# The triangular inverse of a gated delta rule: X of each level as a transpose of XT

## The chip, the core and the metric

The kernel runs on one core of one Trainium2 chip. The metric is the device time of one execution in microseconds; the lower, the better. Three runs of the kernel before gave 1061.08 to 1063.31 us with a median of 1063.28 us.

## What is computed

Two transformer blocks in a row on 256 tokens of width 1024, all in float32. The first has sliding-window attention beside a recurrent unit and a feed-forward part. The second has a block-sparse attention (8 heads) beside a gated delta rule (8 heads of 128), and again a feed-forward part. The change lies in the gated delta rule alone. The reference splits the 256 tokens into chunks of 64; the kernel uses two chunks of 128, which gives the same function. What matters of the reference:

```python
def gated_delta_rule(q, k, v, g, beta):
    ...
    gc = jnp.cumsum(g, axis=-1)
    decay = jnp.exp(jnp.where(causal, gc[..., :, None] - gc[..., None, :], -jnp.inf))
    k_beta = k * beta[..., None]
    a_low = jnp.where(strict, jnp.einsum("bhnid,bhnjd->bhnij", k_beta, k) * decay, 0.0)
    t_mat = a_low + jnp.eye(L, dtype=f32)
    rhs = jnp.concatenate([v * beta[..., None], k_beta * jnp.exp(gc)[..., None]], axis=-1)
    sol = lax.linalg.triangular_solve(t_mat, rhs, left_side=True, lower=True, unit_diagonal=True)
    u = sol[..., :dv]
    w = sol[..., dv:]
    attn = jnp.where(causal, jnp.einsum("bhnid,bhnjd->bhnij", q, k) * decay, 0.0)
    ...
```

## The kernel before

It is written engine by engine; each engine runs its own program in order and waits on semaphores. Weights come from memory in panels of 1 MB through a ring of four slots, two units of 128x1024 to a panel. For float32 accuracy every weight unit is split into two parts that TensorE multiplies at its fast rate: ScalarE copies the high part (`hi`, L601), VectorE subtracts it to get the low part (`lo`, L1044). A unit of projection is eight steps of three matmuls each (L1497 to L1499 or L1503 to L1505). When TensorE has finished a unit, ScalarE copies its result out of PSUM (L800 for the first six of a round) and splits the unit four further on, and VectorE makes that one's low part.

The delta rule has four rounds, one for each pair of heads (`a` = 0 to 3, called first to fourth round here). A round has 21 stages, written by hand for each engine (`gdn_stage`). Between the stages stand projection steps for the next round (for the last: for a gate), as many behind each stage as the table `GDN_WEAVE` says: 9, 8, 4, 6, 4, then one behind each of stages 5 to 16, then 4, 3, 3 and 11. ScalarE and VectorE handle unit `c` behind the stage in which its eighth step falls: unit 3 in stage 5, unit 4 in stage 13, unit 5 in stage 18, none in stages 14 to 17.

The solve is done as a triangular inverse. X is the inverse of (A + 1) for blocks on the diagonal, for four matrices of 128x128 (two chunks, two heads) at once, and XT is its transpose. Level 0 starts in stage 3. Levels 1 to 6 take two stages each and double the blocks:

- odd stage (5, 7, ... 15), "P": TensorE forms A transposed times XT (L1799), two matrices to a group `g`; VectorE masks the result into PM (L1324).
- even stage (6, 8, ... 16), "Z": TensorE forms X transposed times PM (L1810), and in levels 1 to 5 also PM transposed times X (L1814), a third product. VectorE subtracts half of the first from XT and half of the second from X (`grow`, L1289). The next P waits for XT, the next Z for X and PM.

Other work stands in the same stages. ScalarE: `out_root` (the root of the output norm of the round before, L909 to L912) in stage 7, `decays` of the next round (L898, L901, L902) in stage 13, `out_hi` (L917) in stage 14, the gate's silu (L888, with a load of its function table) in stage 15, and then the copies between the state products: u0 (L870, stage 17), S1 (L873), vn (L876), o (L891). VectorE: `prepare` (L1344, L1346) in stage 8, `exponents` (L1350, L1351) in stage 10, `out_rows` (L1358, L1360) in stage 11, `out_lo` (L1366) in stage 14. TensorE: `g_rows` (L1855) in stage 9, `out_transposes` (L1861) in stage 13, the products with X (L1820, L1822) in stage 17, and L1827 in stage 18, which waits for u0. The convolution of the next round runs on POOL (L564, L567) behind the raw copies. `gdn_stage` has the new lines at the stages named.

Of the kernel before, what the change touches and what calls it, by code (L numbers as in the profile page):

```python
# [26 lines left out]
ACT = mybir.ActivationFunctionType  # L27
AX = mybir.AxisListType.X

P = 128  # L30
# [14 lines left out]
PAIRS = HEADS2 // 2  # L45
# [159 lines left out]
def build(nc, A):  # L205
    ctx = ExitStack()
    with ctx:
# [3 lines left out]
        def sem(name):  # L211
            return ctx.enter_context(nc.semaphore(name))
# [27 lines left out]
        def carve(state, *shape):  # L240
# [149 lines left out]
            sem(n) for n in ("gdn_v_rows", "gdn_k_rows", "gdn_kk_products", "gdn_kq_products", "gdn_attn_ready", "gdn_q_scaled", "gdn_kv_scaled", "gdn_A_ready", "inv_identity_ready",  # L390
                             "inv_x0_ready", "inv_xt0_in_psum", "inv_xt0_ready"))

        lv_p, lv_pm, lv_z, lv_x, lv_xt = ([sem(f"{n}{g}") for g in range(2)] for n in (
            "inv_p_in_psum", "inv_p_ready", "inv_z_in_psum", "inv_x_ready", "inv_xt_ready"))
        vb_out, sz_out, os_out = sem("gdn_vb_ready"), sem("gdn_gate_ready"), sem("gdn_o_copied")
        uw_ps, u0_out, nw_out, so_ps, S1_out, vn_ps, vn_out, o_ps, og_out, y_out, yT_ps, yb_hi, yb_lo = (
            sem(n) for n in ("gdn_u_w", "gdn_u0", "gdn_nwT", "gdn_state_ps", "gdn_state", "gdn_vnew_ps", "gdn_vnew",
# [184 lines left out]
        def _(act):  # L582
# [255 lines left out]
            def gdn_stage(s, a):  # L838
# [35 lines left out]
                if s == 19:  # L874
                    act.wait_ge(vn_ps, a + 1)
                    act.activation(vn, acc[:, 3, 256:512].rearrange("p (j n) -> p j n", j=2), ACT.Copy).then_inc(vn_out, 1)  # L876
                if s == 7 and not (isinstance(a, int) and a == 0):
                    out_root(a - 1)
                if s == 14 and not (isinstance(a, int) and a == 0):
                    out_hi(a - 1)  # L880
                if s == 13 and not (isinstance(a, int) and a == PAIRS - 1):
                    decays(a + 1)
                if s == 15:
                    act.wait_ge(emptied[0], along(EMPTIED0, 2 * P_GDN + 8, 8, a))
                    act.wait_ge(emptied[1], along(EMPTIED1, 2 * P_GDN + 8, 8, a))
                    if not (isinstance(a, int) and a == 0):
                        act.wait_ge(y_out, a)
                    act.activation(sz, zr, ACT.Silu).then_inc(sz_out, 1)  # L888
# [16 lines left out]
            def out_root(b):  # L905

                act.wait_ge(os_out, b + 1)
                for pr in range(4):
                    ins = act.activation(junk[:, 512 + pr * P:640 + pr * P], o_s[:, pr, :], ACT.Square, accum_out=st[:, pr:pr + 1])  # L909
                ch.link(ins)  # L910
                ch.link(act.activation(st[:, 4:8], st[:, 0:4], ACT.Ln, bias=eps[:, 0:1], scale=1.0 / P))
                act.activation(st[:, 4:8], st[:, 4:8], ACT.Exp, scale=-0.5).then_inc(og_out, 1)  # L912
# [116 lines left out]
        def _(dve):  # L1029
# [253 lines left out]
            def half_blocks(x, n, odd):  # L1283

                return x.rearrange("p r (q two b) -> p (r q) two b", two=2, b=1 << n)[:, :, odd, :]

            def grow(x, n, odd, z):
                v = half_blocks(x, n, odd)
                return TT(v, v, z, ALU.subtract)  # L1289

            def gdn_stage(s, a):
# [34 lines left out]
                if 5 <= s < 17 and s % 2 == 0:  # L1326
                    lv = (s - 5) // 2 + 1
                    for g in range(2):
                        dve.wait_ge(lv_z[g], a * 6 + lv)
                        z = acc[:, 1 + g, :].rearrange("p (r n) -> p r n", r=4)  # L1330
                        grow(XT_[:, 2 * g:2 * g + 2, :], lv, 1, half_blocks(z[:, 0:2, :], lv, 1)).then_inc(lv_xt[g], 1)
                        if lv < 6:
                            grow(X_[:, 2 * g:2 * g + 2, :], lv, 0, half_blocks(z[:, 2:4, :], lv, 0)).then_inc(lv_x[g], 1)
                if s == 17:
                    dve.wait_ge(uw_ps, a + 1)
                    TS(nwT, acc[:, 0, 0:256].rearrange("p (j n) -> p j n", j=2), -1.0, None, ALU.mult).then_inc(nw_out, 1)
# [146 lines left out]
        def _(pe):  # L1483
# [273 lines left out]
            def gdn_stage(s, a):  # L1757
# [30 lines left out]
                if 5 <= s < 17 and s % 2 == 1:  # L1788

                    lv = (s - 5) // 2 + 1  # L1790
                    if lv == 1:
                        pe.wait_ge(xt0_out, a + 1)
                        pe.wait_ge(kv_out, a + 1)
                        pe.wait_ge(attn_out, a + 1)
                    for g in range(2):
                        if lv > 1:
                            pe.wait_ge(lv_xt[g], a * 6 + (lv - 1))
                        for j in range(2):
                            last = mm(acc[:, 3 * g, j * P:(j + 1) * P], A_[:, 2 * g + j, :], XT_[:, 2 * g + j, :], start=True, stop=True)  # L1799
                        last.then_inc(lv_p[g], 1)  # L1800
                if 5 <= s < 17 and s % 2 == 0:

                    lv = (s - 5) // 2 + 1
                    for g in range(2):
                        pe.wait_ge(lv_pm[g], a * 6 + lv)
                        if lv > 1:
                            pe.wait_ge(lv_x[g], a * 5 + (lv - 1))
                        for j in range(2):
                            pr = 2 * g + j
                            last = mm(acc[:, 1 + g, j * P:(j + 1) * P], X_[:, pr, :], PM_[:, pr, :], start=True, stop=True)  # L1810
                        if lv < 6:
                            for j in range(2):
                                pr = 2 * g + j
                                last = mm(acc[:, 1 + g, (2 + j) * P:(3 + j) * P], PM_[:, pr, :], X_[:, pr, :], start=True, stop=True)  # L1814
                        last.then_inc(lv_z[g], 1)
                if s == 17:
                    for g in range(2):
# [154 lines left out]
```

## Time and profile before

| | |
|---|---|
| median of three runs | 1063.28 us (1061.08 to 1063.31) |
| span of the profiled execution | 1062.7 us; only the span is recorded for it, 0.6 us under the median |
| TensorE busy | 933.3 us (88%), 6486 instructions |
| VectorE busy | 580.4 us (55%) |
| ScalarE busy | 515.9 us (49%) |
| POOL busy | 139.2 us (13%) |
| mean granted TensorE clock | 0.949 |
| the four rounds | about 520 to 738 us from the span's start, 54 us each |

Each row of a timeline has the start in us from the span's start, the duration, engine, line, operation, output and inputs, shape and the number of merged instructions. The bracket is the idle time of that engine before it and what ended it. A float32 matmul of 128x128 leaves two records, a float32 transpose one. Matmuls are pipelined: a group's printed duration has the tail of its last one in it, so the distance between starts says what a group occupies. All tiles carved out of one large buffer are called R, PSUM is ps.

### The profile page before, as it was taken

The numbers are of one execution on the slowest core, as the hardware profiler recorded it, in microseconds if no ns is written. First come the engines' busy times: TensorE is split into PE (matmuls) and PEld (weight loads), VectorE is DVE, ScalarE is ACT, GpSimd is POOL, SyncE is SP. The second block draws the span as 40 slices with busy tenths as digits, with TensorE's granted clock in tenths as the row PEclk, the third lists the DMA queues.
The fourth block names the chain that finished last, engine by engine and source line by source line (L and its number), as shares of the span: only waits on it lengthen the run. The fifth ranks groups of instructions, "written<-read, shape, count | busy, mean of one in ns | idle before, by whom it ended". The sixth has DMA issues, their size and how long they took to land.

```text
span 1062.7 us, 16705 instructions
## 1 busy us (share of the span) xinstructions
PE 933.3 (88%) x6486; PEld 856.1 (81%) x6486; DVE 580.4 (55%) x842; ACT 515.9 (49%) x859; POOL 139.2 (13%) x131
## 2 busy tenths in 40 slices
PE   1598769999999789988699898998988999999967
PEld 1596548999897788988688888888976799999946
DVE  1376554555556555558463737363656455555454
ACT  2458453444445544555636464636336444444442
POOL 4000021000000000007555545300000000000000
PEclk9699889999999889999899999999989899999969
DMA  9643227565556244444122222222554465555601
GB/s 191 210 160 119 79 57 158 188 197 193 169 192 198 75 131 152 124 152 144 62 73 84 76 80 79 80 80 80 180 188 134 142 192 170 194 197 170 231 34 39
DMA packets 106876, 144.88 MB, mean 136 GB/s; under 512 B 3104, under 2 KB 94368, under 8 KB 106704
## 3 DMA queue, kind: packets, MB, share of 16 engines
q1 hardware_dynamic: 104304, 137.37, 40.7%
q0 software_dynamic: 2208, 6.25, 2.8%
q10 hardware_dynamic: 320, 0.66, 0.2%
q8 instruction: 30, 0.49, 0.2%
q14 instruction: 14, 0.11, 0.0%
HBM read 143.22 MB, written 1.05 MB: 136 GB/s over the span
## 4 chain that ended last, share of the span: by engine, by line
PE 73%; DVE 11%; ACT 9%; DMA 3%; issue 3%; POOL 1%; SPq 0%; ACTq 0%; DVEq 0%; POOLq 0%
PE ps L1497 13%; PE ps L1499 13%; PE ps L1498 13%; PE ps L1503 8%; PE ps L1505 8%; PE ps L1504 8%; DVE wl L1044 3%; DMA w_raw<-in_w_in_dram 3%; ACT wh L601 3%; PE ps L1799 2%; PE ps L1810 1%; DVE xTl L1072 1%; PE ps L1688 1%; PE ps L1814 1%; PE ps L1631 1%
## 5 line engine op out<-in xcount | busy, mean ns | idle before, releaser
L1044 DVE TENSOR_TENSOR wl<-w_raw,wh 128x1024 fp32r<-128x1024 f32 x258 | 322.8, 1256 | 354.8 <-ACT wh L601 354.2
L1497 PE MATMUL ps<-xTh,wh 128*128 128x256 f32 (+1 forms) x1160 | 339.2, 292 | 29.3 <-DVE xTl L1072 20.3
L601 ACT ACTIVATE wh<-w_raw 128x1024 fp32r<-128x1024 f32 x258 | 270.5, 1052 | 133.1 <-PE ps L1505 85.7
L1498 PE MATMUL ps<-xTl,wh 128*128 128x256 f32 (+1 forms) x1160 | 329.2, 284 | 0.0
L1499 PE MATMUL ps<-xTh,wl 128*128 128x256 f32 (+1 forms) x1160 | 328.9, 284 | 0.0
L1497 PEld LDWEIGHTS ps<-xTh,wh 128*128 128x128 f32 x1160 | 222.4, 192 | 34.1 <-DVE xTl L1072 20.7
L1498 PEld LDWEIGHTS ps<-xTl,wh 128*128 128x128 f32 x1160 | 221.3, 191 | 2.6 <-issue 1.7
L1499 PEld LDWEIGHTS ps<-xTh,wl 128*128 128x128 f32 x1160 | 222.2, 192 | 0.0
L1503 PE MATMUL ps<-wh,y 128*128 128x512 f32 x224 | 88.9, 397 | 4.0 <-DVE y L1452 4.0
L1505 PE MATMUL ps<-wh,y 128*128 128x512 f32 x224 | 88.6, 395 | 0.0
L1504 PE MATMUL ps<-wl,y 128*128 128x512 f32 x224 | 88.1, 393 | 0.0
L564 POOL TENSOR_TENSOR R<-R 128x512 f32<-128x512 f32 x12 | 13.2, 1103 | 390.6 <-ACT R L800 390.6
L1503 PE MATMUL ps<-wh,xTh 128*128 128x256 f32 (+3 forms) x184 | 56.9, 311 | 7.6 <-DVE xTl L1072 2.7
L1504 PE MATMUL ps<-wl,xTh 128*128 128x256 f32 (+3 forms) x184 | 55.4, 303 | 0.0
L564 POOL TENSOR_TENSOR gain<-R 128x512 f32<-128x512 f32 x36 | 54.9, 1524 | 2.8
L1505 PE MATMUL ps<-wh,xTl 128*128 128x256 f32 (+3 forms) x184 | 55.2, 302 | 0.0
L1503 PEld LDWEIGHTS ps<-wh,y 128*128 128x128 f32 x224 | 42.8, 191 | 12.3 <-DVE y L1452 4.3
L1505 PEld LDWEIGHTS ps<-wh,y 128*128 128x128 f32 x224 | 42.6, 190 | 9.5
L1504 PEld LDWEIGHTS ps<-wl,y 128*128 128x128 f32 x224 | 42.7, 191 | 8.4
L567 POOL TENSOR_TENSOR R<-R,gain 128x512 f32<-128x512 f32 x36 | 43.6, 1210 | 2.8
L1503 PEld LDWEIGHTS ps<-wh,xTh 128*128 128x128 f32 (+1 forms) x184 | 34.7, 189 | 10.9 <-issue 5.5
L752 ACT ACTIVATE R<-ps 128x256 f32<-128x256 f32 x32 | 12.3, 383 | 59.6 <-PE ps L1499 59.6
(331 smaller groups left out, 1337.7 us busy)
## 6 DMA issues: line engine op xcount, KB each, us to landing
w_raw<-in_w_in_dram SPq DMA_DIRECT2D x43, 1024.0 KB, 5.2
w_raw<-in_w_ff_dram SPq DMA_DIRECT2D x32, 1024.0 KB, 5.4
w_raw<-in_w_ffn_gate_dram SPq DMA_DIRECT2D x11, 1024.0 KB, 5.3
w_raw<-in_w_ffn_up_dram SPq DMA_DIRECT2D x11, 1024.0 KB, 5.4
w_raw<-in_w_ffn_down_dram SPq DMA_DIRECT2D x11, 1024.0 KB, 4.9
w_raw<-in_w_out_dram SPq DMA_DIRECT2D x8, 1024.0 KB, 4.8
w_raw<-in_w_proj_a_dram SPq DMA_DIRECT2D x4, 1024.0 KB, 5.0
w_raw<-in_w_proj_b_dram SPq DMA_DIRECT2D x4, 1024.0 KB, 4.9
```

Source lines behind the costliest of these rows:

```text
L564: ins = pool.tensor_tensor(cvt if tap else y, x, w, ALU.mult)
L567: ins = pool.tensor_tensor(y, y, cvt, ALU.add)
L601: act.activation(split_view(wh, pu % UNITS, layout), raw_unit(SLOT[p], j, layout), ACT.Copy).then_inc(w_hi, 1)
L752: act.activation(hid_t[:, j, :], fm[:, j, 0:S], ACT.Relu).then_inc(emptied[j], 1)
L1044: TT(split_view(wl, pu % UNITS, layout), raw_unit(SLOT[p], j, layout), split_view(wh, pu % UNITS, layout).bitcast(F32), ALU.subtract).then ...
L1497: mm(out, wh_, xh, start=first, stop=False)
L1498: mm(out, wh_, xl, start=False, stop=False)
L1499: return mm(out, wl_, xh, start=False, stop=last)
L1503: mm(out, xh, wh_, start=first, stop=False, skip_group_check=not group)
L1504: mm(out, xh, wl_, start=False, stop=False, skip_group_check=not group)
L1505: return mm(out, xl, wh_, start=False, stop=last, skip_group_check=not group)
L1799: last = mm(acc[:, 3 * g, j * P:(j + 1) * P], A_[:, 2 * g + j, :], XT_[:, 2 * g + j, :], start=True, stop=True)
```

## The change

In levels 1 to 5 the third product (PM transposed times X) and VectorE's update of X are gone. Instead TensorE, in the odd stages of levels 2 to 6 behind the P products, transposes the four matrices of XT into the half of the PSUM bank that the third product used, two to a semaphore, and ScalarE copies each group of two into X, 128x256 at a time; Z of that level waits for the copy as it waited for the update. On ScalarE three steps move to make room: `out_root` from stage 7 to stage 4, `decays` from 13 to 16, the silu from 15 to 16, behind the decays.

```diff
--- before.py
+++ after.py
@@ -390,8 +390,8 @@
             sem(n) for n in ("gdn_v_rows", "gdn_k_rows", "gdn_kk_products", "gdn_kq_products", "gdn_attn_ready", "gdn_q_scaled", "gdn_kv_scaled", "gdn_A_ready", "inv_identity_ready",
                              "inv_x0_ready", "inv_xt0_in_psum", "inv_xt0_ready"))
 
-        lv_p, lv_pm, lv_z, lv_x, lv_xt = ([sem(f"{n}{g}") for g in range(2)] for n in (
-            "inv_p_in_psum", "inv_p_ready", "inv_z_in_psum", "inv_x_ready", "inv_xt_ready"))
+        lv_p, lv_pm, lv_z, lv_t, lv_x, lv_xt = ([sem(f"{n}{g}") for g in range(2)] for n in (
+            "inv_p_in_psum", "inv_p_ready", "inv_z_in_psum", "inv_x_in_psum", "inv_x_ready", "inv_xt_ready"))
         vb_out, sz_out, os_out = sem("gdn_vb_ready"), sem("gdn_gate_ready"), sem("gdn_o_copied")
         uw_ps, u0_out, nw_out, so_ps, S1_out, vn_ps, vn_out, o_ps, og_out, y_out, yT_ps, yb_hi, yb_lo = (
             sem(n) for n in ("gdn_u_w", "gdn_u0", "gdn_nwT", "gdn_state_ps", "gdn_state", "gdn_vnew_ps", "gdn_vnew",
@@ -874,13 +874,18 @@
                 if s == 19:
                     act.wait_ge(vn_ps, a + 1)
                     act.activation(vn, acc[:, 3, 256:512].rearrange("p (j n) -> p j n", j=2), ACT.Copy).then_inc(vn_out, 1)
-                if s == 7 and not (isinstance(a, int) and a == 0):
+                if s == 4 and not (isinstance(a, int) and a == 0):
                     out_root(a - 1)
+                if 7 <= s < 17 and s % 2 == 1:
+                    for g in range(2):
+                        act.wait_ge(lv_t[g], a * 5 + (s - 5) // 2)
+                        act.activation(X_[:, 2 * g:2 * g + 2, :], acc[:, 1 + g, 256:512].rearrange("p (j n) -> p j n", j=2),
+                                       ACT.Copy).then_inc(lv_x[g], 1)
                 if s == 14 and not (isinstance(a, int) and a == 0):
                     out_hi(a - 1)
-                if s == 13 and not (isinstance(a, int) and a == PAIRS - 1):
+                if s == 16 and not (isinstance(a, int) and a == PAIRS - 1):
                     decays(a + 1)
-                if s == 15:
+                if s == 16:
                     act.wait_ge(emptied[0], along(EMPTIED0, 2 * P_GDN + 8, 8, a))
                     act.wait_ge(emptied[1], along(EMPTIED1, 2 * P_GDN + 8, 8, a))
                     if not (isinstance(a, int) and a == 0):
@@ -1329,8 +1334,6 @@
                         dve.wait_ge(lv_z[g], a * 6 + lv)
                         z = acc[:, 1 + g, :].rearrange("p (r n) -> p r n", r=4)
                         grow(XT_[:, 2 * g:2 * g + 2, :], lv, 1, half_blocks(z[:, 0:2, :], lv, 1)).then_inc(lv_xt[g], 1)
-                        if lv < 6:
-                            grow(X_[:, 2 * g:2 * g + 2, :], lv, 0, half_blocks(z[:, 2:4, :], lv, 0)).then_inc(lv_x[g], 1)
                 if s == 17:
                     dve.wait_ge(uw_ps, a + 1)
                     TS(nwT, acc[:, 0, 0:256].rearrange("p (j n) -> p j n", j=2), -1.0, None, ALU.mult).then_inc(nw_out, 1)
@@ -1798,6 +1801,11 @@
                         for j in range(2):
                             last = mm(acc[:, 3 * g, j * P:(j + 1) * P], A_[:, 2 * g + j, :], XT_[:, 2 * g + j, :], start=True, stop=True)
                         last.then_inc(lv_p[g], 1)
+                    if lv > 1:
+                        for g in range(2):
+                            for j in range(2):
+                                last = pe.transpose(acc[:, 1 + g, (2 + j) * P:(3 + j) * P], XT_[:, 2 * g + j, :], ident)
+                            last.then_inc(lv_t[g], 1)
                 if 5 <= s < 17 and s % 2 == 0:
 
                     lv = (s - 5) // 2 + 1
@@ -1808,10 +1816,6 @@
                         for j in range(2):
                             pr = 2 * g + j
                             last = mm(acc[:, 1 + g, j * P:(j + 1) * P], X_[:, pr, :], PM_[:, pr, :], start=True, stop=True)
-                        if lv < 6:
-                            for j in range(2):
-                                pr = 2 * g + j
-                                last = mm(acc[:, 1 + g, (2 + j) * P:(3 + j) * P], PM_[:, pr, :], X_[:, pr, :], start=True, stop=True)
                         last.then_inc(lv_z[g], 1)
                 if s == 17:
                     for g in range(2):
```

TensorE's order in the second and third round, from P of level 5 to P of level 6 (L1799 P, L1861 output transposes, L1497 to L1499 the projection step that ends unit 4, L1810 and L1814 Z). Before:

```order
L1799 MATMUL ps<-R 128x128 x4
L1861 MATMUL ps<-cst,R 128x128 x4
L1497 MATMUL ps<-xTh,wh 128x256
L1498 MATMUL ps<-xTl,wh 128x256
L1499 MATMUL ps<-xTh,wl 128x256
L1805 REGISTER_ALU
L1807 REGISTER_ALU
L1810 MATMUL ps<-R 128x128 x2
L1814 MATMUL ps<-R 128x128 x2
L1810 MATMUL ps<-R 128x128 x2
L1814 MATMUL ps<-R 128x128 x2
```

The same place with the change (L1802 P, L1807 the new transposes, L1865 output transposes, L1818 Z):

```order
L1802 MATMUL ps<-R 128x128 x4
L1807 MATMUL ps<-cst,R 128x128 x4
L1865 MATMUL ps<-cst,R 128x128 x4
L1500 MATMUL ps<-xTh,wh 128x256
L1501 MATMUL ps<-xTl,wh 128x256
L1502 MATMUL ps<-xTh,wl 128x256
L1813 REGISTER_ALU
L1815 REGISTER_ALU
L1818 MATMUL ps<-R 128x128 x4
```

Four transposes stand between P and the output transposes, ahead of the step, and four of the eight Z matmuls are gone.

ScalarE's order in the second and third round from unit 4's copy to u0's copy L870 (L917 `out_hi`, L888 silu). Before:

```order
L902 ACTIVATE R<-R 128x128
L604 REGISTER_ALU
L800 ACTIVATE R<-ps 128x256
L601 ACTIVATE wh<-w_raw 128x1024
L917 ISA
L917 ACTIVATE y<-ps 128x512
L884 ISA
L885 REGISTER_ALU
L888 ACT_TABLE_LOAD
L888 ACTIVATE R<-R 128x512
L870 ACTIVATE R<-ps 128x256
L873 ACTIVATE R<-ps 128x256
```

With the change (L882 the new copies of X, L903 to L907 `decays`, L893 silu, L922 `out_hi`), from unit 4's copy down to the first of the decays:

```order
L800 ACTIVATE R<-ps 128x256
L601 ACTIVATE wh<-w_raw 128x1024
L922 ISA
L922 ACTIVATE y<-ps 128x512
L881 REGISTER_ALU
L882 ACTIVATE R<-ps 128x256 x2
L902 REGISTER_ALU
L903 ACTIVATE R<-ps 128x256
L906 ACTIVATE R<-R 128x128
```

and from the last of the decays down to u0's and S1's copies:

```order
L907 ACTIVATE R<-R 128x128
L889 ISA
L890 REGISTER_ALU
L893 ACT_TABLE_LOAD
L893 ACTIVATE R<-R 128x512
L870 ACTIVATE R<-ps 128x256
L873 ACTIVATE R<-ps 128x256
```

The last copies of X, the whole of the decays and the table load with the silu now stand in one row ahead of L870; before, the decays stood ahead of unit 4's copy.

## Rows read from the trace of the kernel before

**Rows 1.** The page: the chain of work that ended last, by engine.

```profile
PE 73%; DVE 11%; ACT 9%; DMA 3%; issue 3%; POOL 1%; SPq 0%; ACTq 0%; DVEq 0%; POOLq 0%
```

**Rows 2.** Windows, second round: us; PE, PEld, DVE, ACT, POOL busy; clock; DMA share; GB/s.

```profile
577.00:631.00 54.00, 49.51 (x400) 46.67 (x400) 31.07 (x64) 28.04 (x61) 28.29 (x22) 1.00 0.24 75
```

**Rows 3.** Timeline, TensorE, fourth round, level 3: start, us, engine, line, operation.

```profile
704.80 1.05 PE L1799 MATMUL ps<-R 128*128 128x128 f32 x8
...
706.05 0.60 PE L1810 MATMUL ps<-R 128*128 128x128 f32 x4
...
707.75 0.37 PE L1497 MATMUL ps<-xTh,wh 128*128 128x256 f32 x1
...
708.19 1.05 PE L1799 MATMUL ps<-R 128*128 128x128 f32 x8
```

**Rows 4.** Timeline, second round, level 1 to level 2; idle time in brackets.

```profile
590.43 0.38 ACT L800 ACTIVATE R<-ps 128x256 f32<-128x256 f32 x1 [2.95 <-PE ps L1499]
...
591.80 1.27 DVE L1044 TENSOR_TENSOR wl<-w_raw,wh 128x1024 fp32r<-128x1024 f32 x1 [1.29 <-ACT wh L601]
...
592.99 0.87 DVE L1289 TENSOR_TENSOR R<-R,ps 128x128 f32<-128x128 f32 x4
...
593.32 1.16 PE L1799 MATMUL ps<-R 128*128 128x128 f32 x8 [0.78 <-DVE R L1289]
```

**Rows 5.** Timeline, second round, levels 4 to 6.

```profile
601.79 0.87 DVE L1324 TENSOR_TENSOR R<-ps,cst 128x256 f32<-128x256 f32 x2 [0.32 <-PE ps L1799]
...
604.69 1.16 PE L1799 MATMUL ps<-R 128*128 128x128 f32 x8
...
605.69 0.60 PE L1861 MATMUL ps<-cst,R 128*128 128x128 f32 x4
...
606.04 0.36 PE L1497 MATMUL ps<-xTh,wh 128*128 128x256 f32 x1
...
609.52 1.16 PE L1799 MATMUL ps<-R 128*128 128x128 f32 x8 [0.73 <-DVE R L1289]
```

**Rows 6.** Timeline, second round: decays, silu, and u0's copy.

```profile
600.17 0.38 ACT L898 ACTIVATE R<-ps 128x256 f32<-128x256 f32 x1 [6.67 <-DVE R L1351]
...
600.45 0.39 ACT L901 ACTIVATE R<-R 128x128 f32<-128x128 f32 x1
...
602.50 0.39 ACT L902 ACTIVATE R<-R 128x128 f32<-128x128 f32 x1
...
607.91 0.59 ACT L917 ACTIVATE y<-ps 128x512 f32 x1
...
608.51 1.28 ACT L888 ACT_TABLE_LOAD   x1
...
609.81 0.63 ACT L888 ACTIVATE R<-R 128x512 f32<-128x512 f32 x1
...
613.91 0.39 ACT L870 ACTIVATE R<-ps 128x256 f32<-128x256 f32 x1 [3.47 <-PE ps L1822]
...
615.13 0.61 PE L1827 MATMUL ps<-R 128*128 128x128 f32 x4
```

**Rows 7.** Timeline, fourth round: four transposes and the copy behind them.

```profile
694.46 0.60 PE L1786 MATMUL ps<-cst,R 128*128 128x128 f32 x4
...
695.09 0.60 ACT L867 ACTIVATE R<-ps 128x512 f32<-128x512 f32 x1 [0.16 <-PE ps L1786]
```

**Rows 8.** Timeline, TensorE, first round: P of level 6, and L1827.

```profile
555.21 1.16 PE L1799 MATMUL ps<-R 128*128 128x128 f32 x8 [0.73 <-DVE R L1289]
...
560.47 0.61 PE L1827 MATMUL ps<-R 128*128 128x128 f32 x4
```

**Rows 9.** Timeline and windows, the stretch behind the last round.

```profile
738.56 0.66 PE L1861 MATMUL ps<-cst,R 128*128 128x128 f32 x4 [1.87 <-DVE R L1360]
...
740.43 0.55 PE L1497 MATMUL ps<-yTh,wh 128*128 128x256 f32 x1 [1.21 <-DVE R L1407]
...
741.00:745.00 4.00, 4.00 (x25) 4.00 (x25) 2.40 (x3) 2.52 (x3) 0.00 (x0) 0.67 0.00 0
```

## The prediction

> **What bounds the kernel now.** I began with the chain that ended last. It lies on TensorE for 73% of the span, with 11% on VectorE and 9% on ScalarE [rows 1]: most of the time is matrix work, and removing matrix work helps where nothing else is late. The change touches only the four rounds of the delta rule, so I next read the windows: in the second round TensorE has work 49.5 of 54 us, with the full clock granted (1.00 of 2.4 GHz) [rows 2]. Then I read the timeline of one level of the inverse where nothing waits, level 3 of the fourth round [rows 3]. From one P product to the next it is 3.39 us (704.80 to 708.19): the P products, one projection step, 1.70 us for the Z products (706.05 to 707.75; 16 records, since a 128x128 f32 matmul leaves two), one more step of 0.44. TensorE is the bound there. It is not the bound everywhere. Before level 2 it stands 0.78 us, since VectorE's update of XT queues behind a weight split (L1044), which waited for ScalarE's L601 [rows 4]. It stands as long before level 6 for the same reason [rows 5]. In level 4 VectorE sets the pace already: masks at 601.79, behind them the output rows of the round before and the update, and P of level 5 at 604.69 [rows 5]. So a gain in TensorE's work has to survive three places with another owner.
>
> **TensorE's work.** Removed: the third product (L1814), 4 matmuls, 8 records, half of the 1.70 us of Z, 0.85 to 0.89 us in levels 1 to 5 of each round. Added: 4 transposes in levels 2 to 6. A f32 128x128 transpose leaves one record: the four of L1861 take 0.35 us to the next instruction [rows 5]; behind other f32 products, where the pause at a switch of kind is not saved, I take 0.44. Per round 5 x 0.89 - 5 x 0.44 = 2.25 us less work, 9.0 us over four. This is not the forecast.
>
> **The new X copies.** ScalarE's copies of 128x256 take 0.39 us (L870) and follow one another by 0.28 (600.17 to 600.45, the step in the exponentials' train, too) [rows 6]. They start 0.03 us after the transposes' modelled end (694.46 + 0.60, 695.09) [rows 7]. From a level's P: 0.9, two transposes 0.1 + 0.27, copy 0.39, release 0.04: X is there about 1.72 us on, and Z of group 0 would start at 0.90 + 0.36 + 0.44 = 1.70. So the copies are just in time and a quiet level becomes 2.95 to 3.0 us instead of 3.39.
>
> **Where the gain survives, second round** (starts of P relative to now):
> - P2: 0. ScalarE's raw copy and split wait for the step in stage 5, which does not move; the update still starts at 592.99, P2 at 593.32 [rows 4]. The 0.89 us removed from level 1 only lengthens the stall from 0.78 to about 1.7.
> - P3: -0.45, TensorE bound (level 2 minus 0.89 plus 0.44).
> - P4: about -0.7 and not -0.9; VectorE's exponents of the next round follow the g rows, which the transposes push back by 0.44 (an estimate: the last 0.2 is theirs).
> - P5: about -0.65. From the masks (601.79) to P5 (604.69) it is 2.90 us of VectorE's work [rows 5], all still there, since X's update was not what P5 waited for.
> - Stage 13: the transposes now stand ahead of the step that completes unit 4, so the step's lead is 0.65 - 0.44 = 0.2. From that step (606.04) to P6 (609.52) it is 3.48 us through L800, L601, L1044 and the update [rows 5], unchanged. P6: -0.2.
> - Level 6 has transposes (+0.44) but lost nothing: the lead is gone at Z6.
>
> Without output rows of an earlier round, the first round keeps about 0.4 more: P6 at -0.6. The fourth keeps about -0.4 at P6.
>
> **ScalarE behind level 6.** This is the term that decides. Decays (2.72 us, 600.17 to 602.50 + 0.39) and the gate's silu (table load 1.28, silu 0.63) now run in stage 16, behind the last X copies, and u0's copy (L870), for which PE L1827 waits, stands behind all of it. Now they lie where ScalarE is idle, and L870 starts at 613.91, 1.2 us before L1827 needs it [rows 6]. Counted from P6 after the change: P 1.00, first two transposes 0.38, wait 0.03, two copy starts 0.28 + 0.28, decays 2.72, load and silu 1.28 + 0.63, u0's copy 0.39, release 0.04, less 0.08 overlap: L1827 at P6 + 6.95. By TensorE alone it would be P6 + 5.6 (609.52 to 615.13) + 0.25. So: second round 6.95 - 5.61 - 0.20 = **+1.14 us**; third the same; first 6.95 - 5.26 (555.21 to 560.47 [rows 8]) - 0.60 = **+1.09**. The fourth has no decays: 4.2 us from P6, no wait, and P6's lead less the transposes, about -0.1. Behind L1827 all is as it was: unit 5's copies, the convolution on POOL and the next round all hang on that step and shift with it. A late dt or sz costs nothing: they are read from stage 3 and stage 11 of the next round.
>
> **out_root** to stage 4 costs nothing: it takes 1.8 us of ScalarE, which idles 2.95 us before L800 at 590.43 [rows 4]. If that cover were gone, unit 3's split, and with it P2, would be late.
>
> **A table switch.** In the rows silu starts 1.30 us after its load began, and the load begins at the end of the activation before (607.91 + 0.59, 608.51) [rows 6], so I take 1.28 and nothing more.
> The Trainium skill (ScalarE: Activation LUTs, "What ACT_TABLE_LOAD costs") gives about 1283 ns for the load and 1380 ns of drain for each switch. By that the three waits would be 1.38 us longer each, an estimate of about 7.5 us for the sum; the load's length agrees with the trace, the drain does not show in it.
>
> **Sum:** 1.09 + 1.14 + 1.14 - 0.1 = +3.3 us on this execution's span of 1062.7. The median of the runs is 1063.28, 0.6 above that span; on the median it is **1066.6**. The bounds: transposes 0.35 or 0.44 (0.1 a round at P6 in each direction), the copies' start and the sequencer's register work for the new waits (0 to 0.3 a round), the overlap: +2 to +4.8.
>
> **Rivals.**
> 1. *The u0 wait is mostly covered* (no change). It would need ScalarE to reach the decays a microsecond earlier, as when P6 keeps the whole lead of 0.65 or more in each round. For it: the first round comes near. Against it: the transposes stand ahead of unit 4's step. Then 3 x 0.3 to 0.6: +1 to +1.8, about 1064.7. Chance 0.19.
> 2. *Faster: TensorE stays the bound.* If VectorE, freed of one of two updates in five levels (0.2 us each of two), takes the splits and updates early enough, and silu and decays fit under the four steps of stage 17, then only level 1's 0.89 is lost: 9.0 - 4 x 0.89 = 5.4 us less, 1057.9. It decides at L1827: it holds only if u0 is ready within 5.8 us of P6. For it: VectorE and ScalarE are busy little over half of the round [rows 2]. Against it: both are in order, and the splits wait for ScalarE, not for VectorE's time. Chance 0.08.
> 3. *The clock falls.* TensorE stands more: 1.7 us before P2, some 1.7 before P6, 1.1 before L1827. In this trace the stalls of 0.8 us inside the rounds left the clock at 1.00 [rows 2], while after the round's end two waits of 1.87 and 1.21 us, with only four transposes between, were followed by 4 us at 0.67 [rows 9]. Such a fall costs 4 x 0.33 = 1.3 us; once a round, 5.3 us on top of 3.3: 1071.9. Against it: between the new stalls stand full products and steps. Chance 0.08.
> The Trainium skill (TensorE: Matmul & The Clock Gate, "PE-mode transpose") says that transposes do not count as TensorE being busy, which speaks against putting them in a product's place; [rows 9] fits that but has two waits as well and cannot separate them.
>
> **The numbers.** The forecast has 0.65. Within 0.2% (2.1 us, about what a measurement of this kernel can tell from no change) fall rival 1 and the edge of the forecast: same 0.20. Faster is rival 2 and noise: 0.09. Slower: 0.71. The range takes in the forecast's bounds and rival 1, with a microsecond for the runs' own spread (1061.08 to 1063.31): 1062 to 1070.5; rivals 2 and 3 lie outside.
>
> **What would show it.** In the profile of the changed kernel: L1827 waits about 1 us for ACT L870 in three rounds and not in the fourth; silu (table load) directly before L870; P of level 2 waits about 1.7 us for the update, P of level 6 about as long; Z of levels 2 to 6 hardly waits for the X copies; the quiet levels last 3.0 us; the clock stays 1.00. I am wrong if L870 starts within 5.5 us of P6, if Z waits for X in each level by more than 0.2 us, or if the rounds are shorter.

## The result and the profile after

The change made the kernel slower: 1068.34 us median (1067.00 to 1069.81, 7 runs) against 1062.09 for the kernel before (7 runs), a ratio of 1.0051 with an interval of 1.0037 to 1.0065. That is 5.4 us, between 3.9 and 6.9. The forecast was +3.3 us, 1066.6 us on the median of three runs known then.

The page of the changed kernel shows less matrix work and a longer span. TensorE is busy 925.5 us, 7.8 less than before, and its share of the chain fell from 73% to 69%, while ScalarE's rose from 9% to 11%:

```profile
PE 925.5 (87%) x6406; PEld 845.6 (79%) x6406; DVE 574.4 (54%) x802; ACT 527.9 (49%) x899; POOL 139.5 (13%) x131
...
PE 69%; DVE 12%; ACT 11%; issue 3%; DMA 3%; POOL 1%; SPq 0%; ACTq 0%; DVEq 0%; POOLq 0%
```

The matrix work became less (a round lost 40 records of products and got 20 of transposes), and waits took its place. Below, P1 to P6 are the starts of the P products of levels 1 to 6 (L1799 before, L1802 with the change), and L1827 stands for the first product behind u0, which is L1831 in the changed kernel and has other line numbers in the kernels of the experiments. Who waited for whom on TensorE between 570 and 625 us, about the second round (total us, times, longest):

```profile
PE ps L1802 <- DVE R L1294: 3.6, 3, 1.7
PE ps L1831 <- ACT R L870: 0.9, 1, 0.9
```

First, P of level 2 in the second round, the place of [rows 4] (L1049 is the low part, L1294 the update, L1802 P):

```profile
594.08 1.27 DVE L1049 TENSOR_TENSOR wl<-w_raw,wh 128x1024 fp32r<-128x1024 f32 x1 [1.29 <-ACT wh L601]
595.27 0.47 DVE L1294 TENSOR_TENSOR R<-R,ps 128x128 f32<-128x128 f32 x2
...
595.60 1.16 PE L1802 MATMUL ps<-R 128*128 128x128 f32 x8 [1.68 <-DVE R L1294]
```

The stall of TensorE ahead of P2 grew from 0.78 to 1.68 us. These 0.90 us are all of the product removed from level 1: P1 to P2 is 4.41 us in both kernels. Second, levels 5 and 6 of that round, the place of [rows 5] (L1807 the new transposes, L1865 the output transposes):

```profile
606.41 1.16 PE L1802 MATMUL ps<-R 128*128 128x128 f32 x8 [0.28 <-DVE R L1294]
...
607.41 0.60 PE L1807 MATMUL ps<-cst,R 128*128 128x128 f32 x4
...
607.84 0.60 PE L1865 MATMUL ps<-cst,R 128*128 128x128 f32 x4
...
611.67 1.16 PE L1802 MATMUL ps<-R 128*128 128x128 f32 x8 [1.63 <-DVE R L1294]
```

P5 to P6 is 5.26 us, against 4.83: the transposes push back the step that ends unit 4, and with it the split and the update. Third, ScalarE's queue ahead of u0's copy, the place of [rows 6]:

```profile
613.09 0.66 ACT L882 ACTIVATE R<-ps 128x256 f32<-128x256 f32 x2 [2.44 <-PE ps L1807]
...
613.63 0.39 ACT L903 ACTIVATE R<-ps 128x256 f32<-128x256 f32 x1
...
615.94 0.39 ACT L907 ACTIVATE R<-R 128x128 f32<-128x128 f32 x1
...
616.35 1.28 ACT L893 ACT_TABLE_LOAD   x1
617.65 0.63 ACT L893 ACTIVATE R<-R 128x512 f32<-128x512 f32 x1
618.18 0.37 ACT L870 ACTIVATE R<-ps 128x256 f32<-128x256 f32 x1
618.60 0.71 PE L1831 MATMUL ps<-R 128*128 128x128 f32 x4 [0.90 <-ACT R L870]
```

From P6 (611.67) to L1831 (618.60) it is 6.93 us; the forecast was 6.95. ScalarE has no idle time between the last X copies and u0's. TensorE's wait for u0 is there in three rounds (0.84, 0.90, 0.89 us) and not in the fourth, where L1831 starts at 727.38, 5.93 us after its P6.

**A measure for the rest.** The spans of single profiles differ outside the rounds: the first P product of the first round starts anywhere from 532.7 to 536.3 us. So I also give, for each kernel, the time from that start to the start of the first product behind u0 in the fourth round. For the two kernels these are (L1799 and L1827 before, L1802 and L1831 after) 186.71 and 191.31 us; the text calls this time "the rounds". Before:

```profile
535.38 1.13 PE L1799 MATMUL ps<-R 128*128 128x128 f32 x8 [0.53 <-DVE R L1311]
...
722.09 0.61 PE L1827 MATMUL ps<-R 128*128 128x128 f32 x4
```

After:

```profile
536.07 1.13 PE L1802 MATMUL ps<-R 128*128 128x128 f32 x8 [0.66 <-DVE R L1316]
...
727.38 0.61 PE L1831 MATMUL ps<-R 128*128 128x128 f32 x4
```

In the table a number is that of the experiment. The last column has the six steps of the second round: P1 to P2, P2 to P3 and so on to P6, and P6 to L1827.

| kernel | ratio to before (interval) | median us | first P to last L1827 | steps of the second round |
|---|---|---|---|---|
| before | | 1062.09 | 186.71 | 4.41 3.55 4.28 3.54 4.83 5.61 |
| the change | 1.0051 (1.0037 to 1.0065) | 1068.34 | 191.31 | 4.41 3.20 3.96 3.65 5.26 6.93 |
| 1: change, decays in 12 | 1.0006 (0.9993 to 1.0020) | 1064.23 | 187.88 | 4.41 3.20 3.96 3.65 5.26 5.86 |
| 5: change, silu in 14 | 1.0055 (1.0038 to 1.0072) | 1069.44 | 192.77 | 4.42 3.20 3.96 3.65 5.26 6.42 |
| 2: before, moves only | 1.0007 (0.9995 to 1.0020) | 1064.44 | 186.77 | 4.41 3.55 4.28 3.54 4.83 5.60 |
| 3: before, low parts later | 0.9975 (0.9964 to 0.9985) | 1060.52 | 184.67 | 3.46 4.53 4.28 3.54 3.93 6.03 |
| 4: change, decays in 12, low parts later | 0.9879 (0.9860 to 0.9898) | 1049.56 | 174.32 | 2.57 3.40 3.96 3.65 3.47 6.02 |
| 6: before, low parts behind masks | 0.9961 (0.9946 to 0.9976) | 1059.83 | 183.26 | 3.47 4.63 4.38 3.54 3.94 5.57 |
| 7: change, decays in 12, low parts behind masks | 0.9904 (0.9884 to 0.9924) | 1055.00 | 177.00 | 2.57 4.41 4.06 3.65 3.47 5.76 |
| 8: as 4, transposes twice | 0.9910 (0.9892 to 0.9927) | 1054.90 | 178.15 | 2.57 3.41 4.40 3.65 3.91 6.03 |
| 9: as 4, decays in 16 | 0.9903 (0.9886 to 0.9919) | 1053.89 | 177.26 | 2.57 3.39 3.96 3.65 3.47 6.83 |
| 10: as 4, transposes by group | 0.9877 (0.9861 to 0.9894) | 1050.85 | 174.47 | 2.57 3.39 3.96 3.87 3.46 6.03 |

The kernel before had medians of 1063.3 to 1063.6 beside the experiments.

### The profile page after: what moved, and what is told of

It is laid out like the page before. It is cut to its first block, busy times and chain, and to the rows that moved or that the text cites. A ratio compares the mean times of both kernels' runs of the same rounds, so it can differ in the third digit from the quotient of the medians.

```text
span 1068.0 us, 16555 instructions
## 1 busy us (share of the span) xinstructions
PE 925.5 (87%) x6406; PEld 845.6 (79%) x6406; DVE 574.4 (54%) x802; ACT 527.9 (49%) x899; POOL 139.5 (13%) x131
## 4 chain that ended last, share of the span: by engine, by line
PE 69%; DVE 12%; ACT 11%; issue 3%; DMA 3%; POOL 1%; SPq 0%; ACTq 0%; DVEq 0%; POOLq 0%
PE ps L1500 12%; PE ps L1502 12%; PE ps L1501 12%; PE ps L1506 8%; PE ps L1508 8%; PE ps L1507 8%; DVE wl L1049 3%; DMA w_raw<-in_w_in_dram 3%; ACT wh L601 3%; PE ps L1802 2%; PE ps L1691 1%; DVE xTl L1077 1%; PE ps L1818 1%; PE ps L1634 1%; ACT junk L609 1%
## 5 line engine op out<-in xcount | busy, mean ns | idle before, releaser
L1049 DVE TENSOR_TENSOR wl<-w_raw,wh 128x1024 fp32r<-128x1024 f32 x258 | 324.0, 1261 | 359.7 <-ACT wh L601 359.2
```

The costliest lines, as they stand in the source:

```text
L1049: TT(split_view(wl, pu % UNITS, layout), raw_unit(SLOT[p], j, layout), split_view(wh, pu % UNITS, layout).bitcast(F32), ALU.subtract).then ...
```

## The experiments

### 1. The change with the decays in stage 12

```diff
-                if s == 16 and not (isinstance(a, int) and a == PAIRS - 1):
+                if s == 12 and not (isinstance(a, int) and a == PAIRS - 1):
                     decays(a + 1)
```

> The change as made, with one step moved: ScalarE's decays of the next round in stage 12 instead of stage 16 (the silu stays in 16). Theory (ScalarE's queue ahead of u0's copy makes the wait): L1831 (the first product behind u0) no longer waits; its waits of 0.84, 0.90 and 0.89 us in the profile of the change and 0.11 us of slower restart each go away, 3.0 us less than the change: about +2 us against the kernel before, ratio 1.001 to 1.003. Rival (the loss comes from the transposes and X copies themselves): within 1 us of the change, ratio 1.004 or more.

Measured: 1.0006, and 3.4 us less in the rounds (187.88 for 191.31), a little more than the 3.0 expected. ScalarE's rows in the second round:

```profile
601.06 0.39 ACT L903 ACTIVATE R<-ps 128x256 f32<-128x256 f32 x1
...
603.37 0.40 ACT L907 ACTIVATE R<-R 128x128 f32<-128x128 f32 x1
604.16 0.66 ACT L882 ACTIVATE R<-ps 128x256 f32<-128x256 f32 x2 [0.40 <-PE ps L1807]
...
611.40 0.63 ACT L893 ACTIVATE R<-R 128x512 f32<-128x512 f32 x1
612.66 0.39 ACT L870 ACTIVATE R<-ps 128x256 f32<-128x256 f32 x1 [0.63 <-PE ps L1826]
```

The decays now lie between the X copies of levels 4 and 5, with 0.40 us to spare, and u0's copy waits for TensorE again, not the other way round. This one queue was three quarters of the loss in the rounds, 3.4 of 4.6 us. What is left, 1.2 us, lies where a level got transposes and kept no gain: in the second round level 5 takes 5.26 for 4.83 us and P6 to L1827 5.86 for 5.61.

### 2. The kernel before with the moves alone

```diff
-                if s == 7 and not (isinstance(a, int) and a == 0):
+                if s == 4 and not (isinstance(a, int) and a == 0):
                     out_root(a - 1)
...
-                if s == 13 and not (isinstance(a, int) and a == PAIRS - 1):
+                if s == 16 and not (isinstance(a, int) and a == PAIRS - 1):
                     decays(a + 1)
-                if s == 15:
+                if s == 16:
```

> The kernel before, with only the three steps moved (output root to stage 4, decays and silu to stage 16); three products and both updates as before. Theory: ScalarE is free from 608.5 us in the second round, so decays, table load and silu (4.6 us) end near 613.1, before u0's copy at 613.9: no wait, ratio 1.000 within 0.001. The moves cost only together with the X copies ahead of them. Rival (the moves alone are the loss): ratio 1.003 or more and L1827 waits for L870.

Measured: 1.0007, and 186.77 for 186.71 us in the rounds. In a second round without X copies ScalarE gets to the decays early, and u0's copy still waits 0.88 us for its product:

```profile
605.74 0.39 ACT L898 ACTIVATE R<-ps 128x256 f32<-128x256 f32 x1
...
608.47 1.28 ACT L888 ACT_TABLE_LOAD   x1
609.76 0.63 ACT L888 ACTIVATE R<-R 128x512 f32<-128x512 f32 x1
611.27 0.39 ACT L870 ACTIVATE R<-ps 128x256 f32<-128x256 f32 x1 [0.88 <-PE ps L1822]
```

The moves cost nothing by themselves. They cost because the last X copy holds them back until TensorE has transposed XT in level 6.

### 3. and 4. VectorE's low parts behind the next update, before and with the change

Units 3 and 4 get their low part behind the update of the stage that follows, instead of ahead of it; `out_lo` goes to stage 16. Kernel 3 is the kernel before with this edit, kernel 4 the change with decays in stage 12 and the same edit.

```diff
-                if s == 14 and not (isinstance(a, int) and a == 0):
+                if s == 16 and not (isinstance(a, int) and a == 0):
                     out_lo(a - 1)
...
+                held = []
                 for s, done in enumerate(finished(weave)):
                     stage(s, a)
-                    for c in done:
-                        unit(c, fu + c, 8, a, pair)
+                    for c in held + list(done):
+                        if stage is gdn_stage and s in (5, 13):
+                            held = held + [c]
+                        else:
+                            unit(c, fu + c, 8, a, pair)
+                            held = [x for x in held if x != c]
```

> The kernel before, with VectorE's low parts of units 3 and 4 put behind the update of the next stage, and out_lo from stage 14 to 16. Theory (VectorE's queue, where the split stands ahead of the update, makes the stalls ahead of P2 and P6): these stalls of 0.78 and 0.73 us per round go, 6.0 us less than the kernel before, ratio 0.993 to 0.996. Rival (the stalls come back in the next stage, since the split now stands ahead of the masks): within 0.2% of before.

> The change with decays in stage 12 (as in the first kernel of this call) and the same moves of VectorE's low parts and out_lo. Theory: the stalls ahead of P2 and P6 (1.68 and 1.63 us per round, 13.2 us) go as well as the u0 waits (3.0 us): 14 to 16 us less than the change, ratio 0.988 to 0.992 against before, and 3 to 5 us under the same deferral without the transposes (per round 5 x 0.83 us of products removed and 5 x 0.59 added, 4.8 us over four). Rival (transposes cost as much as the products they replace): no faster than the deferral alone.

Measured without the transposes: 0.9975, 2.0 us less in the rounds instead of 6.0. The rival was right in part. P2 comes 0.95 us earlier, and then Z of level 2 waits for the masks that stand behind the split:

```profile
591.36 1.56 DVE L1044 TENSOR_TENSOR wl<-w_raw,wh 128x1024 fp32r<-128x1024 f32 x1
...
592.84 0.74 DVE L1324 TENSOR_TENSOR R<-ps,cst 128x256 f32<-128x256 f32 x2
...
593.39 0.71 PE L1815 MATMUL ps<-R 128*128 128x128 f32 x4 [0.88 <-DVE R L1324]
```

Measured with the transposes: 0.9879 (0.9860 to 0.9898), 1049.56 us, 17 us less in the rounds than the change as made, and 14 us under the kernel before. It is faster than both kernels, and gained more than the 14 to 16 us expected over the change. Here P and four transposes stand ahead of the same Z, and the masks are nearly in time, 0.21 us late for 0.88:

```profile
587.68 1.27 DVE L1049 TENSOR_TENSOR wl<-w_raw,wh 128x1024 fp32r<-128x1024 f32 x1 [0.18 <-ACT wh L601]
...
588.87 0.74 DVE L1329 TENSOR_TENSOR R<-ps,cst 128x256 f32<-128x256 f32 x2
...
589.41 1.15 PE L1823 MATMUL ps<-R 128*128 128x128 f32 x8 [0.21 <-DVE R L1329]
```

So VectorE's order, a split ahead of an update, is what swallowed the product removed. The step from P1 to P2 shows it: 4.41 us before and with the change, 3.46 in kernel 3 and 2.57 in kernel 4, where the 0.89 us of the removed product now count.

The difference between kernels 3 and 4, 10.4 us in the rounds, is more than the 3 to 5 expected. The count of matrix work left out that P and the transposes also give VectorE time: between 500 and 745 us Z waits 5.0 us for the masks in kernel 3 and 0.7 in kernel 4. The two kernels also differ in the places of ScalarE's steps, but TensorE's waits for ScalarE are 7.6 and 7.7 us in that stretch, so these places do not make the difference.

### 5. The change with the silu ahead, in stage 14

```diff
-                if s == 16:
+                if s == 14:
                     act.wait_ge(emptied[0], along(EMPTIED0, 2 * P_GDN + 8, 8, a))
```

> The change as made, but the silu with its table load back ahead, in stage 14 behind out_hi (decays stay in stage 16). Theory (the wait is the length of ScalarE's queue between the last X copies and u0's copy, whatever stands in it): without the 1.9 us of load and silu the decays end at about 616.4 in the second round and u0's copy is ready before TensorE wants it at 617.7: no wait, the same time as with the decays in stage 12, 0.999 to 1.003 against before. Rival (the decays, not the queue's length, make the wait, or the silu ahead delays the X copies of level 6): ratio 1.003 or more.

Measured: 1.0055, no better than the change. A miss: I had counted the queue as 1.9 us shorter, but between the silu and the exponentials ScalarE has to load another table, so the load stays in the queue:

```profile
573.08 1.28 ACT L841 ACT_TABLE_LOAD   x1
...
613.08 0.66 ACT L882 ACTIVATE R<-ps 128x256 f32<-128x256 f32 x2 [0.49 <-PE ps L1807]
...
613.76 1.28 ACT L903 ACT_TABLE_LOAD   x1
...
617.68 0.36 ACT L870 ACTIVATE R<-ps 128x256 f32<-128x256 f32 x1
618.09 0.71 PE L1831 MATMUL ps<-R 128*128 128x128 f32 x4 [0.40 <-ACT R L870]
```

The wait for u0 is 0.40 for 0.90 us here, and the silu that begins the next round (L841) needs its table back. Between 500 and 745 us TensorE waits 7.0 us for ScalarE's squares (L844), which stand behind that silu, against 4.0 in kernel 1, and from the first L1831 to the next round's P1 it is 29.53 us for 28.55 with the change. So the order of the kinds of function in the queue counts beside its length. That the wait goes when the queue is short enough is shown by kernel 1 alone.

### 6. and 7. The low parts one stage later still, behind the masks

Kernel 6 is the kernel before, kernel 7 the change with decays in stage 12; both have this edit in place of the one to `held` above, and `out_lo` in stage 16 as well.

```diff
+                    if stage is gdn_stage and s in (5, 13):
+                        held = list(done)
+                        done = ()
+                    if s in (7, 15):
+                        done, held = held + list(done), []
```

> The kernel before with the low parts of units 3 and 4 put one stage later still, behind the masks of levels 2 and 6 (out_lo again in 16). In the first deferral Z of levels 2 and 6 waited 5.0 us in all for the masks behind the split. Theory: that wait goes and nothing takes its place: 5 us less than the first deferral's rounds, about 1056 to 1058 us, ratio 0.993 to 0.996. Rival (the split then makes the update behind it late, P of level 3 waits): ratio as the first deferral, 0.997 to 0.998.

> The change with decays in stage 12 and the low parts one stage later still, as in the kernel above. There the masks made Z wait 0.7 us in all. Theory: at most 0.7 us less than the first deferral of the change (1049.6), and 5 to 8 us under the same deferral of the kernel before: what the transposes are worth where TensorE is the bound. By 5 x 0.83 less 5 x 0.59 per round it would be 4.8 us. Rival (most of the 11 us between the two first deferrals was the transposes): still 9 us or more under it.

Measured: 0.9961 without and 0.9904 with the transposes. Both expectations of the time missed. Kernel 6 is 1.4 us under kernel 3 in the rounds where 5 were expected, and kernel 7 is 2.7 above kernel 4 where up to 0.7 less was expected. The rival of the first held in the main: the wait moved once more. The split now stands ahead of `prepare` and the update of level 2, and P3 waits 1.02 us in the kernel without transposes:

```profile
591.88 1.55 DVE L1044 TENSOR_TENSOR wl<-w_raw,wh 128x1024 fp32r<-128x1024 f32 x1
...
593.36 1.01 DVE L1344 COPY R<-R 128x24 f32 x1
...
595.08 1.16 PE L1805 MATMUL ps<-R 128*128 128x128 f32 x8 [1.02 <-DVE R L1289]
```

With the transposes this place is worse than the first deferral (177.00 for 174.32 us in the rounds; level 2 takes 4.41 for 3.40). Between kernels 6 and 7 the transposes are worth 6.3 us in the rounds, within the 5 to 8 expected, less than the 10.4 between kernels 3 and 4 and more than the count of 4.8.

### 8. Every transpose made twice

```diff
-                            for j in range(2):
+                            for j in (0, 1, 0, 1):
                                 last = pe.transpose(acc[:, 1 + g, (2 + j) * P:(3 + j) * P], XT_[:, 2 * g + j, :], ident)
```

> The first deferral of the change with every transpose of XT made twice into the same place (80 more transposes in all, the result is the same). It measures the transposes by themselves. Theory (four cost 0.44 us of TensorE): 20 x 0.44 = 8.8 us more than without, plus a few tenths where the X copies are later, less what hides in the waits of P: 7 to 10 us more, about 1057 to 1060. Rival (they cost 0.35 or less, or hide beside the weight loads): under 7 us more.

Measured against kernel 4: 5.3 us more by the medians, 3.8 us in the rounds, under the 7 to 10 expected. By the number the rival holds, but the steps show another reason than its own. Four more transposes cost 0.44 us in levels 3 and 5 of the second round (4.40 for 3.96, 3.91 for 3.47), as the theory had it, but only 0.01 in levels 2 and 6, where Z had waited for the masks, and nothing in level 4, where the masks and output rows of VectorE set the pace. In the quiet levels of the first and fourth round it is 0.22 to 0.23 (fourth round, level 3: 3.39 for 3.16), since there a wait of Z for the X copy goes at the same time (experiment 10). Their price is 0.44 where TensorE is the bound, and less wherever it had been waiting. The granted clock stayed at 1.00 through the rounds:

```profile
536.00:715.00 179.00, 170.73 (x1409) 163.41 (x1410) 98.58 (x188) 106.13 (x227) 76.03 (x60) 1.00 0.23 77
```

### 9. The decays back in stage 16, low parts deferred

Kernel 4 with `decays` in stage 16.

> The first deferral of the change (low parts behind the next update, out_lo in 16), but with the decays back in stage 16, as the change has them. Here TensorE reaches level 6 two microseconds earlier in relation to unit 4's split than in the change. Theory: ScalarE's queue behind the last X copies has the same length, and L1836 comes some 6.9 us after P6 instead of 6.02: 0.9 us and 0.1 of restart in three rounds, 3 to 3.5 us more than with the decays in stage 12 (1049.6), about 1053. Rival (unit 4's split and out_hi now also stand ahead and the wait grows): 5 us or more.

Measured: 1053.89 for 1049.56 us, and 2.9 us more in the rounds (177.26 for 174.32), against 3 to 3.5 expected; L1836, the first product behind u0 here, comes 6.83 us after P6 for 6.02. Its waits:

```profile
PE ps L1836 <- ACT R L870: 2.1, 3, 0.8
```

This is the same term, measured a second time in another setting.

### 10. Transposes directly behind their own group's P

```diff
                         last.then_inc(lv_p[g], 1)
-                    if lv > 1:
-                        for g in range(2):
+                        if lv > 1:
                             for j in range(2):
```

> The first deferral of the change with each group's transposes directly behind its own P products instead of behind both. X of group 0 is ready 0.45 us earlier, the masks of group 1 0.22 us later. Theory: Z waits less than 0.1 us for the X copies now, so the time stays within 0.2% of the first deferral, the P starts move by under 0.1 us per level. Rival (the X copies hold Z back in each level): 20 x 0.1 to 0.3 = 2 to 6 us less.

Measured: no difference in the time (0.9877 for 0.9879), but not for the reason I gave. Level 3 of the fourth round became 0.23 us shorter (2.93 for 3.16), and level 4 of the second, which has the output rows, 0.22 us longer (3.87 for 3.65); that the later masks of group 1 make it longer was not tried by itself. So Z did wait for the X copies. In the change as made the rows of that quiet level show it, weight loads (PEld) included:

```profile
709.49 1.06 PE L1802 MATMUL ps<-R 128*128 128x128 f32 x8
...
710.38 0.60 PE L1807 MATMUL ps<-cst,R 128*128 128x128 f32 x4
...
710.80 0.66 ACT L882 ACTIVATE R<-ps 128x256 f32<-128x256 f32 x2 [2.50 <-PE ps L1807]
...
711.05 0.28 PE L1502 MATMUL ps<-xTh,wl 128*128 128x256 f32 x1
711.30 0.97 PEld L1818 LDWEIGHTS ps<-R 128*128 128x128 f32 x8 [0.17 <-issue]
711.33 1.13 PE L1818 MATMUL ps<-R 128*128 128x128 f32 x8
```

Z starts 0.28 us behind the start of the step's last matmul; in kernel 10 the same distance is 0.11 (698.78 to 698.89). The row has both copies; the first takes 0.38 us and ends at 711.18, and Z starts 0.15 us later. In the second and third round the wait is smaller. There Z starts 0.18 us behind the step's last matmul and 0.06 us after the end of the first copy (597.01 + 0.38 = 597.39):

```profile
597.01 0.66 ACT L882 ACTIVATE R<-ps 128x256 f32<-128x256 f32 x2 [2.97 <-PE ps L1807]
...
597.27 0.28 PE L1502 MATMUL ps<-xTh,wl 128*128 128x256 f32 x1
597.45 1.16 PE L1818 MATMUL ps<-R 128*128 128x128 f32 x8
```

Where the 0.15 us of the first and fourth round come from is not shown. That X is loaded as weights is no sufficient reason, since it is so in every round. And where the masks come last, an operand that streams, Z starts 0.05 us after the first of them in the fourth round of the kernel before (718.03 to 718.08) and 0.13 us after it in the second (610.99 to 611.12).

## Why the prediction was right, and where its sizes were off

**Right: the term that decides.** "L1827 at P6 + 6.95" was 6.93, in three rounds and not in the fourth, with the table load and silu directly ahead of u0's copy. Its terms hold one by one, so the sum is no luck: in the second round it is, from P6 to the first X copy, 1.42 us (forecast 1.41), from there to the decays 0.54 (0.56), the decays 2.70 (2.72), from the table load to u0's copy 1.83 (1.83), and from there to L1831 0.42 (0.43). Undone alone (kernel 1) it gives back 3.4 us in the rounds; added alone to the fast version (kernel 9) it costs 2.9.

**Right: the first product's gain is lost.** P2 did not move (4.41 us in both), and the stall became 1.68, where 1.7 was forecast. That VectorE's queue is the cause was an argument then; kernels 3, 4, 6 and 7 show it, since each new place of the split moves the stall to the instruction behind it.

**Right: P6.** In the second round P1 to P6 is 20.48 us for 20.61: 0.13 earlier, forecast 0.2. The stall was 1.63, "some 1.7".

**Right: the table switch.** Load to silu is 1.30 us again (616.35 to 617.65), and the load starts as the last exponential ends. The trace shows nothing between.
The drain that the Trainium skill adds to a switch (ScalarE: Activation LUTs, "What ACT_TABLE_LOAD costs") would have made the sum about 7.5 us; neither the rows nor the rounds' 4.6 us show it.

**Mis-sized: the X copies.** "So the copies are just in time and a quiet level becomes 2.95 to 3.0 us" was the step that failed: quiet levels take 3.15 to 3.27. The forecast took 0.04 us from the copy's end to Z. In the first and fourth round it is 0.15, and Z starts some 0.16 us late in each quiet level; in the second and third it is 0.06, and Z is some 0.06 us late; the reason for the difference is open (experiment 10). With the groups' order changed the quiet level is 2.93, just under the size forecast. In the first and the fourth round, which have more quiet levels, this ate the lead: P6 at -0.19 where -0.6 was forecast (19.64 for 19.83 from P1), and at -0.03 where -0.4 was.

**Left out: the restart.** From L1827 to the next round's P1 it is 28.44 us before and 28.55 after in two of the gaps, 27.14 and 27.29 in the third. From the first to the second pair of products behind u0 it is 0.45 us before (615.13 to 615.58) and 0.55 after the wait (618.60 to 619.15). I had "behind L1827 all is as it was". Over the three gaps this is 0.37 us.

**The sum.** Round by round, from P1 to L1827: +1.48, +1.19, +1.19 and +0.37 us, where I had +1.09, +1.14, +1.14 and -0.1; with 0.37 between the rounds 4.60 us. That lies in the bounds of the sum (+2 to +4.8), 1.3 us above the +3.3 forecast, and nearly all of the 1.3 are the two terms above: 0.4 in the first round, 0.5 in the fourth and 0.37 between the rounds, all in one direction. The measured 5.4 (3.9 to 6.9) is 0.8 more; the interval holds 4.6, and no row shows another cause.

**Rivals.** The first (u0 covered) is refuted by the three waits. The second, TensorE as the bound and 5.4 us less, was not this kernel. Kernel 4 comes near it once entries of VectorE's and ScalarE's queues have changed places, with more gain than the rival had. The third did not come: with stalls of 1.68 us the granted clock of the changed kernel stayed at its upper level, 1.00, through the second round:

```profile
590.00:596.00 6.00, 3.67 (x30) 3.29 (x29) 4.14 (x8) 2.76 (x11) 5.19 (x4) 1.00 0.00 0
...
588.00:643.00 55.00, 47.98 (x381) 44.79 (x382) 28.92 (x53) 30.80 (x70) 27.33 (x23) 1.00 0.23 71
```

That transposes do not count as TensorE being busy, as the Trainium skill has it (TensorE: Matmul & The Clock Gate, "PE-mode transpose"), made no difference here: the clock stayed at 1.00. Products stand about all of them, so no run tests the sentence by itself.

What stays open: how the 10.4 us between kernels 3 and 4 divide between less TensorE work and covered waits. The waits for the masks account for 4.3 us (5.0 less 0.7), which leaves 6.1, near the 6.3 between kernels 6 and 7; but both pairs have waits of their own. The steps of the second round give 0.89 us for level 1, 1.13 for level 2, 0.32 for level 3 and 0.46 for level 5, with 0.11 lost in level 4.

## What to carry to other kernels

Work taken off the busiest engine is worth nothing at a point where the next step waits for another engine's queue: follow, for each wait, the whole in-order queue ahead of the instruction that releases it, and expect the wait to move to whatever stands behind when one entry is moved. Before moving filler work behind a new dependency, add up the queue from there to the next copy that someone waits for; a change that loses by that may be the better one once entries of two queues change places (here 1068.3 us became 1049.6 with the decays earlier on ScalarE and the low parts later on VectorE).

## What the runs showed that I had not expected

- The time from the end of the last operand's copy to the first matmul that waits for it is not one number: 0.15 us from the X copy to Z in the first and fourth round and 0.06 in the second and third, and from the masks to the same Z 0.05 in the fourth and 0.13 in the second. The cause is open.
- Moving a silu between two groups of exponentials cost two more table loads of 1.28 us in each of the three rounds that have decays, one ahead of the decays (L903) and one ahead of the next round's silu (L841) (kernel 5).
- VectorE's copy of 128x24 took 1.01 us in kernel 6 and 0.31 before, and a split 1.55 for 1.27. POOL was at work beside both, but also beside the copy of 0.31 and the split of 1.27 us in the kernel before; the cause is open.
